# One of four weight sums per MLP unit moved from GpSimd to VectorE

## The chip, the cores and the metric

The kernel runs on one core of a Trainium2 chip. The metric is the time of one launch on the device, in microseconds, as the median of three runs.

## The reference, cut to what matters

A transformer stack on 512 tokens of width 1024, all in float32: a first block of two attention layers, then a second block of four layers whose mixers are attention, neighbourhood attention, a convolution module and a Fourier mixer. Each layer of the second block ends in the same MLP, and the change touches nothing else:

```
def sq_relu_mlp(h, w1, w2):
    return jnp.square(jax.nn.relu(h @ w1)) @ w2
...
x = x + ml[5] * sq_relu_mlp(modulate(rms_norm_2(x, norm2_g[i]), ml[3], ml[4]), mlp_w1[i], mlp_w2[i])
```

`w1` is 1024 x 4096 and `w2` 4096 x 1024. In layer 0 the MLP is applied to 256 context tokens too.

## The kernel before, in words

TensorE, VectorE, ScalarE and GpSimd each have one program, written out in full when the kernel is built, and they meet by semaphores. The work is a list of stages. Between most stages every engine has a gate that waits until the others are done with the stage before; TensorE has no gate in front of an MLP.

**An MLP stage** (kind `fast`) multiplies matrices by Strassen's method in Winograd's form: a product of 2 x 2 blocks takes seven block products and not eight. It is cut into units. A unit takes one block of weights out of a ring of three slots in SBUF (2 MB each, filled by SyncE's queue), as four sub-blocks `a11, a12, a21, a22`. The seven products want four sums of them:

- `s1 = a21 + a22`, `s2 = s1 - a11`, `s4 = a12 - s2`, made on VectorE by `weight_sums` (L2415, L2417, L2419), each into a buffer of its own, with a wait for the one before;
- `a11 - a21`, the third sum, made on GpSimd by `third_sum` (L3057), which writes it over `a21` in the ring. It waits for `s1`, since `s1` reads `a21`.

TensorE (L1856) takes a unit's products in the order 1, 5, 2, 6, 3, 7, 4 (`ORDER`), or 1, 2, 5, 6, 3, 7, 4 in a first unit. Product 5 wants `s1`, 6 wants `s2`, 3 wants `s4`, and 7 wants the third sum (`s3_made`). VectorE makes a unit's sums while TensorE is still in the unit before: behind `sum_u2` (L2484), which reads product 6 of that unit, and ahead of `c12` (L2490) and `sum_u3` (L2500). Then come `c21_sum` (L2506) and, in some units, the partial sums for the next layer's modulation (L2587, L2591). In the first unit of each kind VectorE also makes four sums of the activations (`token_sums`, L2438 to L2448). GpSimd's own list in a unit is the third sum of the next unit and then the addition that makes `c22` (L3082).

**The sizes.** Layer 0 has 32 units with sub-blocks of 128x512 elements. Layers 1, 2 and 3 have 16 units each, with sub-blocks of 128x1024. That makes 80 units.

**The start of an MLP.** The first unit's `weight_sums` has nothing ahead of it in its own stage, so it is run in the stage before, as a step named `wsums` behind one residual tile. In layers 1 to 3 that is the last tile but one of the residual additions: VectorE makes the first unit's sums and then adds the last tile (L2633 in layer 1, L2636 and L2637 in layers 2 and 3). Behind the last tile come its squares on ScalarE (L2236), their addition on GpSimd (L3030), the sum over channels on TensorE (L1682), the root on ScalarE (L2245), its inverse on VectorE (L2833, L2834), the spread on TensorE (L1696), the scaling of the second half of the tokens (L2849) with the shift on ScalarE (L2258), and the first activation sum (L2438). In the first unit TensorE goes through product 1, L1682, the first half of product 2, L1696, the second half of product 2, and product 5, which waits for L2438. GpSimd's `third_sum` of a first unit stands behind GpSimd's gate, so it runs when the MLP's stage has begun.

Of the kernel before, what the change touches and what calls it, by code (L numbers as in the profile page):

```python
# [17 lines left out]
ALU = mybir.AluOpType  # L18
# [246 lines left out]
def build_program(nc, dram, out_dram, stages_kept=10000):  # L265
    ctx = ExitStack()
    with ctx:
# [3 lines left out]
        def sem(name):  # L271
            return ctx.enter_context(nc.semaphore(name))
# [84 lines left out]
        product_ready, s_sums, s3_made, t_made = sem("product_ready"), sem("s_sums"), sem("s3_made"), sem("t_made")  # L357
# [7 lines left out]
        stages, blocks = [], []  # L365
# [203 lines left out]
        for c0 in range(0, 2560, 512):  # L569
# [8 lines left out]
        idx_tiles[2].after = [("swap", idx_heads, 0), ("swap", idx_heads, 1)]  # L578
        wi_tiles[-1].after = [("swap", idx_heads, 2)]
        ab_list = [t for _, tiles, _ in ab_groups[1:] for t in tiles]  # L580
        qk_data = ([(QA[:, t], V("qa_g")) for t in range(4)] + [(KA[:, 0], V("ka_g"))]
                   + [(QB[:, t], V("qb_g")) for t in range(4)] + [(KB[:, 0], V("kb_g"))])
# [487 lines left out]
        def shaped(x, u):  # L1070

            x = x[:, 0:u["cols"]]
            return x.rearrange("p (m n) -> p m n", m=2) if u["mt"] == 2 else x
# [390 lines left out]
        def gate(eng, own, s):  # L1464

            for name, sm in stage_of.items():
                eng.wait_ge(sm, s)
            if tables_before[s]:
                eng.wait_ge(tables_in, tables_before[s])
# [917 lines left out]
        def _(dve):  # L2387
# [19 lines left out]
            def weight_sums(u):  # L2407

                a11, a12, a21, a22 = u["blocks"]
                s1, s2, s4 = u["s"]  # L2410
                base = 3 * u["id"]
                dve.wait_ge(weights_in[u["b"] % RING], landed[u["b"]])
                if u["id"] >= 2:
                    dve.wait_ge(product_ready, 7 * u["id"] - 7)
                nc.vector.tensor_tensor(s1, a21, a22, ALU.add).then_inc(s_sums, 1)  # L2415
                dve.wait_ge(s_sums, base + 1)
                nc.vector.tensor_tensor(s2, s1, a11, ALU.subtract).then_inc(s_sums, 1)  # L2417
                dve.wait_ge(s_sums, base + 2)
                nc.vector.tensor_tensor(s4, a12, s2, ALU.subtract).then_inc(s_sums, 1)  # L2419
                sums_ahead[0] = u["id"] + 1  # L2420
# [461 lines left out]
            def next_sums(unit, _):  # L2882
                weight_sums(unit)
# [114 lines left out]
        def _(pool):  # L2998
# [38 lines left out]
            for s, st in enumerate(stages):  # L3037
                if st["kind"] not in ("prep", "norm"):
                    gate(pool, "pool", s)
                if st["kind"] == "norm":  # L3040

                    for k in range(1, st["summed"]):
                        pool.wait_ge(squares_ready, st["sq0"] + k + 1)
                        if k > 1:
                            pool.wait_ge(pool_steps, pool_count)
                        ins = nc.gpsimd.tensor_tensor(st["sq"][:, 0, :], st["sq"][:, 0, :], st["sq"][:, k, :], ALU.add)
                        if k < st["summed"] - 1:
                            ins.then_inc(pool_steps, 1)
                            pool_count += 1
                        else:  # L3050
                            ins.then_inc(sumsq_ready, 1)
                if st["kind"] == "fast":

                    def third_sum(u):
                        a11, _, a21, _ = u["blocks"]
                        pool.wait_ge(s_sums, 3 * u["id"] + 1)
                        nc.gpsimd.tensor_tensor(a21, a11, a21, ALU.subtract).then_inc(s3_made, 1)  # L3057

                    us, tmp = st["units"], st["tmp"]
                    last = us[-1]  # L3060
                    listed = {p: [x for x in last["after"][p] if x[0] == "nsq"] for p in last["order"] if p in last["after"]}
                    third_sum(us[0])
                    for i, u in enumerate(us):
                        if i + 1 < len(us):
                            third_sum(us[i + 1])
                        n_units = u["id"]
                        if u["last"]:
                            for kind, normed, at in listed[1] + listed[2] + listed[4]:
                                sum_squares(normed, *at)
                        if u.get("closes"):  # L3070
                            for kind, normed, at in [x for x in us[-2]["after"][1] if x[0] == "nsq"] + listed[1]:
                                sum_squares(normed, *at)
                        pool.wait_ge(u3_out, n_units + 1)
                        pool.wait_ge(t5_copied, n_units + 1)
                        if u["up"]:
                            to = u["dst"][1][1]
                        else:
                            to = tmp["v"][:, 0:u["cols"]]
                            if n_downs:
                                pool.wait_ge(x22_out, n_downs)  # L3080
                            n_downs += 1
                        nc.gpsimd.tensor_tensor(to, shaped(tmp["u3"], u), shaped(tmp["t5"], u),  # L3082
                                                ALU.add).then_inc(c22_out, 1)
                        if u["last"]:
                            for kind, normed, at in listed[5] + listed[3]:
                                sum_squares(normed, *at)
                        if u.get("closes"):
                            for kind, normed, at in listed[2]:
                                sum_squares(normed, *at)
                    pool.wait_ge(c22_out, us[-1]["id"] + 1)  # L3090
                if "loads_bias" in st:
                    load_bias(0)
                for dst, src, i in st.get("shifts", []):
                    values = st["groups"][-1][1]
                    pool.wait_ge(*values[i].done)
                    pool.dma_start(dst, src).then_inc(shifted_in, 16)
                if st["kind"] == "project":
                    rotations = [x for _, tiles, _ in st["groups"] for t in tiles for x in t.after] + st.get("steps", [])
                    last = None
                    for kind, job, i in rotations:  # L3100
                        if kind == "nsq":
                            sum_squares(job, *i)
                        if kind == "glu":
                            pool.wait_ge(*job.done)
                            u = U[:, i, TAPS // 2:TAPS // 2 + S]
                            nc.gpsimd.tensor_tensor(u, u, SIG[:, i, :], ALU.mult).then_inc(glu_done, 1)  # L3106
                        if kind != "swap":
                            continue
                        data, g, made_by = job.tiles[i]
                        r = job.r[i]  # L3110
                        if last is None:
                            pool.wait_ge(tables_in, tables_before[s] + 16 * len(st["loads"]))
                        if g is not None:
                            pool.wait_ge(yn_ready, job.sp[i] + 1)
                            src = job.yn[:, r % 2, 0:job.n]
                        else:
                            if made_by is not None:
                                pool.wait_ge(*made_by.done)
                            src = data
                        if r >= 2:  # L3120
                            pool.wait_ge(rope_done, r - 1)
                        nc.gpsimd.tensor_tensor(job.t1[:, r % 2, 0:job.n], src, job.cos[0:job.parts, 0:job.n],
                                                ALU.mult).then_inc(cos_ready, 1)
                        last = r + 1
                    if last is not None:
                        pool.wait_ge(cos_ready, last)
                if st["kind"] == "attention" and st["passes"][0]["bias"] is not None:
                    for t in range(1, len(st["passes"])):
                        if t >= 2:
                            pool.wait_ge(bias_used, t - 1)  # L3130
                        load_bias(t)
                pool.sem_inc(stage_of["pool"], 1)
# [89 lines left out]
```

## Time and profile before

| what | value |
|---|---|
| median of three runs | 3859.96 us (3858.89 to 3861.55) |
| span of the profiled execution | 3863.2 us |
| mean granted TensorE clock in it | 0.991 of full speed |
| TensorE matmul, weight load | 3731.4 us (97%), 2529.2 us |
| VectorE, ScalarE, GpSimd | 1986.4 us (51%), 968.1 us, 585.1 us |
| instructions | 42209 |

The span is that of one profiled execution, and no time of its own is given beside it; it is 3.2 us above the median of the runs. Durations below come from that execution. An engine's share of busy time says only how full it is. What a change of its work is worth is read from the waits of the engine that is never idle.

### The profile page before, as it was taken

The numbers are of one execution on the slowest core, as the hardware profiler recorded it, in microseconds if no ns is written. First come the engines' busy times: TensorE is split into PE (matmuls) and PEld (weight loads), VectorE is DVE, ScalarE is ACT, GpSimd is POOL, SyncE is SP. The second block draws the span as 40 slices with busy tenths as digits, with TensorE's granted clock in tenths as the row PEclk, the third lists the DMA queues.
The fourth block names the chain that finished last, engine by engine and source line by source line (L and its number), as shares of the span: only waits on it lengthen the run. The fifth ranks groups of instructions, "written<-read, shape, count | busy, mean of one in ns | idle before, by whom it ended". The sixth has DMA issues, their size and how long they took to land.

```text
span 3863.2 us, 42209 instructions
## 1 busy us (share of the span) xinstructions
PE 3731.4 (97%) x16228; PEld 2529.2 (65%) x16232; DVE 1986.4 (51%) x3470; ACT 968.1 (25%) x2234; POOL 585.1 (15%) x476
## 2 busy tenths in 40 slices
PE   9999999999999999999999899999999999999997
PEld 4458445455554655555644588888568888788886
DVE  3654346644773575564301946663765665344343
ACT  2142215521552312112201622021313111221010
POOL 1001000001000111111202411112422111111111
PEclk9999999999999999999999999999999999999998
DMA  3112331022002132333213314543102454122221
GB/s 138 62 43 89 101 106 60 1 93 72 26 1 64 66 122 96 131 109 109 72 67 81 60 44 165 183 153 109 66 22 99 163 175 153 61 73 84 87 85 43
DMA packets 226949, 341.41 MB, mean 88 GB/s; under 512 B 32256, under 2 KB 100512, under 8 KB 226720
## 3 DMA queue, kind: packets, MB, share of 16 engines
q1 hardware_dynamic: 201552, 320.60, 24.2%
q0 software_dynamic: 6816, 10.01, 1.4%
q10 hardware_dynamic: 18384, 8.11, 0.7%
q8 instruction: 132, 2.16, 0.2%
q14 instruction: 65, 0.53, 0.0%
HBM read 333.03 MB, written 4.06 MB: 87 GB/s over the span
## 4 chain that ended last, share of the span: by engine, by line
PE 88%; DVE 6%; ACT 2%; issue 2%; POOL 1%; DMA 1%; ACTq 0%; DVEq 0%; POOLq 0%
PE psum L1856 43%; PE psum L1603 29%; PE psum L1976 3%; PE psum L1923 3%; PE psum L1953 2%; PE psum L1710 1%; DVE small L2918 1%; DVE arena L2591 1%; ACT arena L2347 1%; POOL arena L3106 1%; PE psum L1632 1%; PE psum L1644 1%; PE psum L1661 1%; ACT arena L2335 1%; PE psum L1550 1%
## 5 line engine op out<-in xcount | busy, mean ns | idle before, releaser
L1603 PE MATMUL psum<-HC,ring 128*128 128x256 f32 (+2 forms) x3184 | 1034.1, 484 | 11.7 <-ACT HC L2258 4.5
L1603 PEld LDWEIGHTS psum<-HC,ring 128*128 128x128 f32 (+1 forms) x3184 | 600.1, 190 | 429.2 <-issue 375.2
L1856 PE MATMUL psum<-arena,ring 128*128 128x256 f32 (+1 forms) x2304 | 604.9, 416 | 6.0 <-ACT arena L2110 6.0
L1856 PEld LDWEIGHTS psum<-arena,ring 128*128 128x128 f32 x2304 | 433.6, 190 | 150.3 <-ACT arena L2110 10.9
L1856 PE MATMUL psum<-arena 128*128 128x256 f32 (+1 forms) x1792 | 472.3, 418 | 0.4
L1856 PE MATMUL psum<-HC,ring 128*128 128x256 f32 (+1 forms) x1792 | 435.6, 396 | 4.4 <-ACT arena L2110 4.4
L1856 PEld LDWEIGHTS psum<-arena 128*128 128x128 f32 x1792 | 340.3, 190 | 114.7 <-ACT arena L2115 0.7
L3057 POOL TENSOR_TENSOR ring<-ring 128x1024 f32<-128x1024 f32 (+1 forms) x80 | 217.2, 2715 | 1213.9 <-DVE arena L2415 1183.1
L1856 PEld LDWEIGHTS psum<-HC,ring 128*128 128x128 f32 x1792 | 338.4, 191 | 80.1 <-ACT arena L2110 5.1
L2591 DVE SCALAR_TENSOR_TENSOR arena<-ring,cond,arena 128x512 f32<-128x512 f32 x448 | 318.6, 749 | 8.0
L2484 DVE TENSOR_TENSOR arena<-psum,arena 128x384 f32<-128x384 f32 (+2 forms) x80 | 44.5, 556 | 378.1 <-PE psum L1856 378.0
L2918 DVE TENSOR_REDUCE small<-psum 128x1 f32<-128x512 f32 (+8 forms) x352 | 186.8, 565 | 92.8 <-PE psum L1935 57.8
L2335 ACT ACTIVATE arena<-psum,small 128x256 f32<-128x256 f32 (+8 forms) x320 | 183.4, 577 | 113.7 <-DVE small L2918 78.9
L3030 POOL TENSOR_TENSOR arena<-arena 128x256 f32<-128x256 f32 (+1 forms) x82 | 68.3, 833 | 926.7 <-ACT arena L2236 924.4
L2419 DVE TENSOR_TENSOR arena<-ring,arena 128x1024 f32<-128x1024 f32 (+1 forms) x80 | 201.7, 2521 | 2.7
L1953 PE MATMUL psum<-ident,arena 128*128 128x128 f32 x984 | 150.2, 282 | 34.9 <-ACT arena L2347 23.6
L1856 PE MATMUL psum<-CX,arena 128*128 128x256 f32 x768 | 175.0, 382 | 5.8 <-DVE CX L2438 5.8
L2063 ACT ACTIVATE arena<-psum 128x512 f32<-128x512 f32 (+4 forms) x124 | 58.7, 476 | 457.9 <-PE psum L1603 452.9
L1856 PEld LDWEIGHTS psum<-CX,arena 128*128 128x128 f32 x768 | 146.9, 192 | 27.1 <-issue 6.9
L2110 ACT ACTIVATE arena<-psum 128x384 f32<-128x384 f32 (+2 forms) x80 | 39.1, 489 | 485.5 <-PE psum L1856 485.5
L2347 ACT ACTIVATE arena<-psum 128x512 f32<-128x512 f32 (+3 forms) x272 | 139.7, 552 | 67.7 <-PE psum L1953 67.4
L1953 PEld LDWEIGHTS psum<-ident,arena 128*128 128x128 f32 x984 | 105.9, 142 | 74.5 <-issue 31.8
(236 smaller groups left out, 3834.1 us busy)
## 6 DMA issues: line engine op xcount, KB each, us to landing
ring<-in_mlp_w SPq DMA_DIRECT2D x64, 2048.0 KB, 8.8
ring<-in_ada_w SPq DMA_DIRECT2D x48, 2048.0 KB, 7.9
ring<-in_na_qkv SPq DMA_DIRECT2D x6, 2048.0 KB, 7.9
ring<-in_ab_in SPq DMA_DIRECT2D x5, 2048.0 KB, 9.3
ring<-in_cd_in SPq DMA_DIRECT2D x4, 2048.0 KB, 10.0
ring<-in_pw SPq DMA_DIRECT2D x8, 1024.0 KB, 6.6
ring<-in_at_qkv SPq DMA_DIRECT2D x3, 2048.0 KB, 10.4
ring<-in_ab_out SPq DMA_DIRECT2D x2, 2048.0 KB, 7.8
```

Source lines behind the costliest of these rows:

```text
L1603: last = nc.tensor.matmul(out, lhs, rhs, start=(k == 0), stop=(k == len(t.pairs) - 1))
L1856: last = nc.tensor.matmul(bank(at, u["T"], u["T"] * m), w[:, i, P * m:P * m + P], x[:, i, :], start=(opens and m == 0 and i == 0), stop=(i ...
L1923: last = nc.tensor.matmul(psum[:, at:at + k1 - k0], p["q"](g, qt * P, qt * P + P), p["k"](g, a * P + k0, a * P + k1), start=(m < 3), stop= ...
L1953: last = nc.tensor.transpose(psum[0:rows, c0:c0 + P], pair["probs"][g][:, k0:k0 + rows], ident[:, :])
L1976: last = nc.tensor.matmul(psum[HD * g:HD * g + HD, at + q0:at + q1], p["v"](g, of[0] if of else kt), chunk["turned"][0:p["krows"], kt, g, ...
L2335: nc.scalar.activation(pair["probs"][g][:, 0:nk + more], psum[:, off:off + nk + more], ACT.Exp, bias=small[:, c:c + 1], accum_out=small[:, ...
L2347: nc.scalar.activation(dst, src, ACT.Copy).then_inc(act_copied, 1)
L2419: nc.vector.tensor_tensor(s4, a12, s2, ALU.subtract).then_inc(s_sums, 1)
L2591: ins = nc.vector.scalar_tensor_tensor(partial[:, v, :], w[:, k, :], cond[:, k, v:v + 1], partial[:, v, :], ALU.mult, ALU.add)
L2918: nc.vector.tensor_reduce(small[:, c:c + 1], psum[:, off:off + nk], AX, ALU.max, negate=True).then_inc(negmax_ready, 1)
L3030: ins = nc.gpsimd.tensor_tensor(total, total, normed.sq[:, k, cols], ALU.add)
L3057: nc.gpsimd.tensor_tensor(a21, a11, a21, ALU.subtract).then_inc(s3_made, 1)
```

## The change

The third sum is issued on VectorE, in `weight_sums`, between `s2` and `s4`, with the same operands, the same place in the ring and the same semaphore. `third_sum` and its two calls are taken out of GpSimd's program. No wait is added.

```diff
@@ weight_sums, VectorE
                 nc.vector.tensor_tensor(s1, a21, a22, ALU.add).then_inc(s_sums, 1)
                 dve.wait_ge(s_sums, base + 1)
                 nc.vector.tensor_tensor(s2, s1, a11, ALU.subtract).then_inc(s_sums, 1)
+                nc.vector.tensor_tensor(a21, a11, a21, ALU.subtract).then_inc(s3_made, 1)
                 dve.wait_ge(s_sums, base + 2)
                 nc.vector.tensor_tensor(s4, a12, s2, ALU.subtract).then_inc(s_sums, 1)
@@ the MLP stages, GpSimd
-                    def third_sum(u):
-                        a11, _, a21, _ = u["blocks"]
-                        pool.wait_ge(s_sums, 3 * u["id"] + 1)
-                        nc.gpsimd.tensor_tensor(a21, a11, a21, ALU.subtract).then_inc(s3_made, 1)
...
-                    third_sum(us[0])
                     for i, u in enumerate(us):
-                        if i + 1 < len(us):
-                            third_sum(us[i + 1])
```

## Rows read from the trace of the kernel before

**Rows 1.** The page: busy time, share of the span and instructions of each engine.

```profile
PE 3731.4 (97%) x16228; PEld 2529.2 (65%) x16232; DVE 1986.4 (51%) x3470; ACT 968.1 (25%) x2234; POOL 585.1 (15%) x476
```

**Rows 2.** TensorE's waits, whole span: line <- releaser, total us, times, longest.

```profile
PE psum L1856 <- ACT arena L2110: 10.5, 12, 4.1
...
PE psum L1856 <- DVE CX L2438: 5.8, 3, 1.9
...
PE psum L1682 <- POOL arena L3030: 1.4, 2, 0.7
```

**Rows 3.** Four MLP stretches (1283.7-1880, 2302-2695, 2945-3341, 3454-3844) summed: us, busy by engine.

```profile
sum 1775.30, PE 1756.44 PEld 1357.03 DVE 954.28 ACT 300.87 POOL 324.99; mean PE 439.11 PEld 339.26 DVE 238.57 ACT 75.22 POOL 81.25
```

**Rows 4.** Groups of the sums: shapes, count, busy us, mean ns, idle before.

```profile
L2419 DVE TENSOR_TENSOR arena<-ring,arena 128x1024 f32<-128x1024 f32 (+1 forms) x80 | 201.7, 2521 | 2.7
...
L2417 DVE TENSOR_TENSOR arena<-arena,ring 128x1024 f32<-128x1024 f32 x48 | 60.0, 1250 | 1.6
...
L2417 DVE TENSOR_TENSOR arena<-arena,ring 128x512 f32<-128x512 f32 x32 | 22.1, 692 | 1.1
```

**Rows 5.** Timeline, one unit of layer 1: start, duration, engine, operation, idle before.

```profile
2311.08 3.39 POOL L3057 TENSOR_TENSOR ring<-ring 128x1024 f32<-128x1024 f32 x1 [14.24 <-DVE arena L2415]
...
2312.30 3.25 DVE L2419 TENSOR_TENSOR arena<-ring,arena 128x1024 f32<-128x1024 f32 x1
```

**Rows 6.** Timeline at the start of layer 2's MLP.

```profile
2937.97 0.54 DVE L2636 TENSOR_SCALAR arena<-psum,vec,mods 128x256 f32<-128x256 f32 x1
...
2939.49 0.72 POOL L3030 TENSOR_TENSOR arena<-arena 128x256 f32<-128x256 f32 x1 [3.79 <-ACT arena L2236]
...
2940.18 2.35 POOL L3057 TENSOR_TENSOR ring<-ring 128x1024 f32<-128x1024 f32 x1
...
2940.36 0.58 PE L1682 MATMUL psum<-mean_d,arena 128*128 128x1 f32 x4 [0.70 <-POOL arena L3030]
...
2940.80 1.97 PE L1856 MATMUL psum<-HC,ring 128*128 128x256 f32 x8
...
2941.57 1.24 DVE L2834 SCALAR_TENSOR_TENSOR sd_rstd<-ident,sd_rstd 128x256 f32<-128x256 f32 x1
...
2942.95 0.67 PE L1696 MATMUL psum<-sd_rstd,mean_d 128*128 128x256 f32 x2 [0.18 <-DVE sd_rstd L2834]
...
2943.66 1.65 DVE L2849 SCALAR_TENSOR_TENSOR HC<-X,sgain,psum 128x256 f32<-128x256 f32 x4 [0.86 <-PE psum L1696]
```

**Rows 7.** Timeline at the start of layer 1's MLP.

```profile
2292.81 0.48 DVE L2633 SCALAR_TENSOR_TENSOR X<-psum,mods,X 128x256 f32<-128x256 f32 x1
...
2293.81 0.72 POOL L3030 TENSOR_TENSOR arena<-arena 128x256 f32<-128x256 f32 x1 [3.26 <-ACT arena L2236]
...
2295.91 1.99 PE L1856 MATMUL psum<-HC,ring 128*128 128x256 f32 x8 [0.35 <-ACT arena L2110]
...
2297.74 0.59 PE L1696 MATMUL psum<-sd_rstd,mean_d 128*128 128x256 f32 x2
...
2298.37 2.05 DVE L2849 SCALAR_TENSOR_TENSOR HC<-X,sgain,psum 128x256 f32<-128x256 f32 x5 [1.25 <-PE psum L1696]
...
2302.00 7.15 PE L1856 MATMUL psum<-CX,arena 128*128 128x256 f32 x32 [1.94 <-DVE CX L2438]
```

**Rows 8.** Timeline ahead of the joint MLP of layer 0.

```profile
1263.56 0.69 DVE L2834 SCALAR_TENSOR_TENSOR sd_rstd<-ident,sd_rstd 128x512 f32<-128x512 f32 x1
...
1265.66 1.02 PE L1696 MATMUL psum<-sd_rstd,mean_d 128*128 128x512 f32 x2
```

**Rows 9.** Timeline inside layer 2's MLP, where a block of weights lands late.

```profile
3232.69 3.26 DVE L2419 TENSOR_TENSOR arena<-ring,arena 128x1024 f32<-128x1024 f32 x1
...
3243.53 3.72 PE L1856 MATMUL psum<-arena,ring 128*128 128x256 f32 x16 [1.33 <-ACT arena L2110]
```

**Rows 10.** Layer 3's MLP start: timeline, then its window: us, busy, PEclk, DMA.

```profile
3454.25 8.83 PE L1856 MATMUL psum<-CX,arena 128*128 128x256 f32 x32 [1.94 <-DVE CX L2438]
...
3454.00:3465.00 11.00, 10.75 (x42) 9.22 (x43) 6.62 (x10) 3.01 (x6) 0.00 (x0) 0.84 0.01 1
```

## The prediction

> **What bounds the kernel now.** I read four views in this order. The page's busy times [rows 1] show TensorE full, VectorE at half and GpSimd at 15%: the change takes work off an engine that is nearly empty and puts it on one with room. The table of windows over the four MLPs [rows 3] shows how closed they are: of 1775.3 us TensorE is busy for 1756.4, and VectorE for 954.3. So work on VectorE costs or gives nothing unless TensorE waits for it. The list of TensorE's waits says where that is [rows 2]. Of the sums themselves there is no row: TensorE never waits for L2415, L2417, L2419 or L3057. The waits that touch VectorE or GpSimd are three for L2438 (5.8 us) and two for L3030 (1.4 us), and the timelines put all five at the starts of the MLPs of layers 1, 2 and 3 [rows 6, 7, 10]. The twelve for L2110 are ScalarE's copy of product 1; one of 4.1 us is at the joint MLP's start, one is 1.33 us long [rows 9], and the other ten share 10.5 - 4.1 - 1.3 = 5.1 us, some 0.5 us each, which is the copy itself. So the change is to be priced at the starts and at that 1.33, and in the other units only if it made something late.
>
> **The units, 80 times.** Added on VectorE: one TENSOR_TENSOR of the form of L2417, 1.25 us for 128x1024 (48 times) and 0.69 us for 128x512 (32 times) [rows 4]. Removed from GpSimd: L3057, 3.39 us in a unit [rows 5]. There is a third effect. L2419 took 3.25 us for what L2417 does in 1.25: it began at 2312.30 and ended at 2315.55, 1.08 us after L3057 ended at 2314.47 [rows 5]. It stood behind GpSimd. Without L3057 it should take 1.25, so the four sums take 4 x 1.25 = 5.0 us, where the three took 1.25 + 1.25 + 3.25 = 5.75 (taking L2415 as L2417). The added instruction is more than paid for. `s1` and `s2` come when they did. The third sum ends 1.25 us after `s2`, 3.75 us after the start of `s1`, where L3057, which begins as `s1` ends, ended 1.25 + 3.39 = 4.64 us after it, and `s4` is 0.75 us earlier. Nothing behind them is later. Over 80 units VectorE's L2419 (201.7 us) becomes two times the busy time of L2417 (2 x 82.1 = 164.2), 37.5 us less in all, and TensorE waited for none of it. I price the units at 0, with one exception.
>
> The exception is [rows 9]. A block landed late, the sums began late, a set of activation sums came behind them, and VectorE reached L2490 so late that ScalarE's queue held up L2110: TensorE waited 1.33 us where the copy alone costs some 0.5. L2419 took 3.26 us there, and two operations of 1.25 stand in its place: VectorE is 0.76 us earlier, and the excess is 0.8. **-0.76 us.** The bounds are 0 (something else ends last there) and -0.8 (the whole excess).
>
> **The starts of layers 1 to 3.** Here the third sum is moved past other work. It was behind GpSimd's gate; now it stands on VectorE ahead of the last residual tile, and the chain square, L3030, L1682, L2833, L2834, L1696, L2849, L2438 hangs on that tile. The tile's addition moves by 1.25 us (L2419 there has no L3057 beside it yet, so nothing comes back in this place).
>
> Layer 2 [rows 6]: L1682 already waits 0.70 us for L3030, so the whole 1.25 goes through, to 2941.61. The first half of product 2 follows 0.44 behind, at 2942.05. L1696 follows that by 2297.74 - 2295.91 = 1.83 where nothing else holds it [rows 7]: 2943.88. In between something is given back: L2834 took 1.24 us beside L3057, and a tile twice as wide took 0.69 without it [rows 8]. By that way L1696 could begin at 2941.57 + 1.25 + 0.69 + 0.14 (as it began 0.14 after L2834 ended) = 2943.65, earlier than 2943.88: TensorE's own order rules. L2849 follows L1696 by 0.63 [rows 7]: 2944.51, against 2943.66. **+0.85.** Everything behind, up to product 5, hangs on L2849. Layer 3 has the same order and the other of the two waits of 0.7 us for L3030 [rows 2]; I take it as the same: **+0.85.**
>
> Layer 1 [rows 7]: L3030 ended at 2294.53, before TensorE wanted it. Now it ends at 2295.78. L1682 follows by 0.15 (as 2940.21 to 2940.36 in [rows 6]) and the product by 0.44: 2296.37 against 2295.91. **+0.46.** Bounds for the three: 0, if some wait behind takes it all up, and 3 x 1.25 = 3.75, if nothing does.
>
> The Trainium skill, page "VectorE: DVE Perf Modes", section "The TRN2 errata", has a table by which a VectorE operation from SBUF to SBUF costs 58 cycles plus its elements at 0.96 GHz, which would be 1.13 us for 1024 elements; the trace has 1.25 from one to the next, so it does not agree here. By the table the starts would cost about 0.1 us less each.
>
> Layer 0 [rows 8]: `weight_sums` runs ahead of L2833. 0.69 us more moves the end of L2834 from 1264.25 to 1264.94; L1696 begins at 1265.66 with no wait, behind a tile of matmuls that covers it. Price 0; were that cover gone, 0.69. GpSimd's L3057 had stood behind the gate there and beside L2445, which no product waited for.
>
> **Sum**: 0.85 + 0.85 + 0.46 - 0.76 = +1.40 us, 0.04% of the span of 3863.2. I take the difference over to the median of the runs: 3859.96 + 1.40 = 3861.4. Here 0.2% is 7.7 us, about what a measurement of this kernel can tell from no change.
>
> **The rivals.**
>
> A. *TensorE's clock falls more often.* Behind the 1.94 us wait of layer 3 the same 32 matmuls took 8.83 us that took 7.15 in layer 1 behind the same wait, and the granted clock of the stretch was 0.84 [rows 10, 7]: part of it at 1.2 and not 2.4 GHz, for 1.68 us. So one of three such idle spells brought a fall. The change makes idle spells of 0.70 us ahead of L1682 into 1.95 in layers 2 and 3, as long as those. For: they are new and long enough. Against: two of three passed without. With one or two more falls: 3861.4 + 1.7 to 3.4 = 3863.1 to 3864.8.
> The Trainium skill, page "TensorE: Matmul & The Clock Gate", Part 1, has the clock set by how busy the engine has been of late; the stretch at 0.84 behind an idle spell agrees, and the level in layer 1 shows that an idle spell of this length need not do it.
>
> B. *Nothing, or a little gained.* L2834 and its neighbours free of L3057 give back what the tile loses, or layer 3's fall does not recur. Against: TensorE's own order comes later than L2834 in my sums. Time: 3859.96 + 0 to -2, 3858 to 3860.
>
> C. *VectorE was the bound after all.* If TensorE's progress hung on VectorE, the 37.5 us would come through: 3822.5. Against: no row in which TensorE waits for a sum, and 1756.4 of 1775.3 us busy [rows 3]. It decides only if a fifth of it (7.7 us) reached TensorE.
> The Trainium skill, page "GPSIMD Engine Reference", section "When to use GPSIMD", would have elementwise work on VectorE because GpSimd is about twice as slow there; the trace agrees (2.35 us for L3057 beside almost nothing, 1.25 on VectorE), but the rule speaks of an instruction and not of the time of this kernel.
>
> D. *Slower by more than 0.2%.* The mechanism of A at its worst: each of the three starts has a fall behind the wait for L1682 and one behind the wait for L2438, six against the one of now, five more: 1.4 + 5 x 1.68 = 9.8, 3869.8. It decides from four more on (1.4 + 6.7 = 8.1). Layer 1's wait for L1682 hardly grows, which speaks against it.
>
> **How the numbers follow.** The forecast 0.50, A 0.25, B 0.18, C 0.03, D 0.04. The first three hold 0.93 within 0.2%. Faster is C, slower D. The range: down to B's middle and half the spread of the runs below it, 3857.6, and up to A's end with the same, 3866.2. It contains both bounds of the starts (+3.75 less nothing, 3863.7) and of the exception.
>
> **What would show it.** Right: L2419 at 1.25 us for 128x1024 and 0.69 for 128x512, no L3057; four sums of 5.0 us; L1682 in layers 2 and 3 waits 1.9 to 2.0 us for L3030, and in layer 1 under 1; L1696 waits for nothing; L2834 at 0.69 or less; L2438 waits still 1.9 us each; the wait at 3243.53 down to about 0.55; VectorE's busy time down by some 37 us, though it has 80 instructions more (82.1 us for the added ones, 119.6 less for L2419). Wrong: a wait of product 5, 6, 3 or 7 for a sum, a residual tile in time with L1682 waiting as before, or a time of more than 7.7 us either way with no wait to show for it, which only another share of half clock would explain.

## The result: 0.13% slower, and the forecast too low

| | kernel before | changed kernel |
|---|---|---|
| median of 20 runs each, in turn | 3861.97 us | 3866.72 us |
| lowest to highest | 3855.91 to 3867.38 | 3861.83 to 3870.76 |
| mean | 3861.93 us | 3866.47 us |
| ratio, 95% interval | | 1.0013 [1.0007, 1.0019] |

The change costs 3866.72 - 3861.97 = 4.75 us, by the interval 2.7 to 7.3. That is under 0.2%, as forecast, but the interval leaves the forecast's +1.40 out, and 3866.72 lies 0.5 us above the range. The miss of 3866.72 - 3861.4 = 5.3 us has two parts: 2.0 is the base (three runs had a median of 3859.96, twenty have 3861.97), and 3.35 is the effect (4.75 against 1.40). Only the second needs an explanation.

The profiled execution of the changed kernel took 3867.0 us, with a span of 3864.8. Its page, busy times first, against [rows 1]:

```profile
span 3864.8 us, 42209 instructions
...
PE 3732.6 (97%) x16232; PEld 2528.8 (65%) x16232; DVE 1931.7 (50%) x3550; ACT 967.6 (25%) x2234; POOL 367.9 (10%) x396
```

VectorE has 80 instructions more and is 54.7 us less busy; GpSimd has 80 fewer and 217 us less. The groups of the four sums, shapes apart (count, busy us, mean ns, idle before), against [rows 4]:

```profile
L2418 DVE TENSOR_TENSOR ring<-ring 128x1024 f32<-128x1024 f32 x48 | 58.5, 1218 | 0.0
...
L2420 DVE TENSOR_TENSOR arena<-ring,arena 128x1024 f32<-128x1024 f32 x48 | 58.4, 1218 | 0.0
...
L2417 DVE TENSOR_TENSOR arena<-arena,ring 128x512 f32<-128x512 f32 x32 | 22.1, 692 | 1.1
```

The groups' engine times add up to 41 us less for the sums (L2419's 201.7 became 80.3, and L2418 is 80.4). Another 13 of the 54.7 are overlap: the third sum and `s4` each start some 0.08 us before the sum ahead of them ends, and the page counts shared time once. L2418 is the third sum, and L2420 is `s4`, which was L2419. It took 3.25 us beside GpSimd's sum [rows 5] and takes 1.22 now. TensorE's waits (total us, times, longest), against [rows 2]:

```profile
PE psum L1856 <- ACT arena L2110: 9.3, 11, 4.1
...
PE psum L1856 <- DVE CX L2439: 4.9, 3, 1.9
...
PE psum L1682 <- POOL arena L3031: 3.9, 3, 1.7
```

No wait names a sum. The waits for ScalarE's copy are 1.2 us less (what that owes to the change is taken up below). The last line is what the change brought: 1.4 us in two waits became 3.9 in three. The timeline has the third of these at layer 1's start, and in layer 2 the wait that was 1.33 us long in [rows 9]:

```profile
2299.28 0.58 PE L1682 MATMUL psum<-mean_d,arena 128*128 128x1 f32 x4 [0.47 <-POOL arena L3031]
...
3247.75 2.43 PE L1856 MATMUL psum<-arena,ring 128*128 128x256 f32 x10 [0.47 <-ACT arena L2110]
```

The start of layer 2's MLP in the timeline, against [rows 6]:

```profile
2938.33 1.63 DVE L2417 TENSOR_TENSOR arena<-arena,ring 128x1024 f32<-128x1024 f32 x1
...
2939.89 1.21 DVE L2418 TENSOR_TENSOR ring<-ring 128x1024 f32<-128x1024 f32 x1
2941.03 1.21 DVE L2420 TENSOR_TENSOR arena<-ring,arena 128x1024 f32<-128x1024 f32 x1
2942.16 0.53 DVE L2637 TENSOR_SCALAR arena<-psum,vec,mods 128x256 f32<-128x256 f32 x1
...
2944.55 0.58 PE L1682 MATMUL psum<-mean_d,arena 128*128 128x1 f32 x4 [1.72 <-POOL arena L3031]
2944.99 2.85 PE L1856 MATMUL psum<-HC,ring 128*128 128x256 f32 x8
2945.76 0.42 DVE L2835 SCALAR_TENSOR_TENSOR sd_rstd<-ident,sd_rstd 128x256 f32<-128x256 f32 x1
2947.64 1.06 PE L1696 MATMUL psum<-sd_rstd,mean_d 128*128 128x256 f32 x2
...
2952.36 7.14 PE L1856 MATMUL psum<-CX,arena 128*128 128x256 f32 x32 [1.55 <-DVE CX L2439]
```

The third sum takes the place 1.14 us long ahead of `s4` (2939.89 to 2941.03), the tile comes later by it, and L1682 waits 1.72 us where it waited 0.70. L2835 takes 0.42 us where it took 1.24. Then comes what the sum of the forecast had not: the eight matmuls at 2944.99 take 2.85 us for 1.97, and L1696 takes 1.06 for 0.59 in the same form of [rows 7]. Two windows of that trace (busy us per engine in the order PE, PEld, DVE, ACT, POOL, then granted clock and DMA) show the clock there and at layer 3's start:

```profile
2945.20:2949.00 3.80, 3.80 (x12) 3.04 (x12) 0.86 (x3) 0.23 (x1) 0.00 (x0) 0.60 0.30 115
...
3451.00:3456.00 5.00, 4.80 (x15) 3.54 (x13) 2.42 (x7) 1.93 (x5) 0.00 (x0) 0.66 0.06 22
```

TensorE never stood still in the first 3.80 us and was granted 0.60 of full speed, so most of it at 1.2 and not 2.4 GHz, right behind the longer wait. The second is a fall at layer 3's start. The kernel before had one in that start too, but behind the wait of 1.94 us for L2438, in product 5 [rows 10]. Here it stands further ahead, behind the new wait:

```profile
3449.55 0.58 PE L1682 MATMUL psum<-mean_d,arena 128*128 128x1 f32 x4 [1.72 <-POOL arena L3031]
3449.98 2.68 PE L1856 MATMUL psum<-HC,ring 128*128 128x256 f32 x8
```

So both new waits of this trace have a fall right behind them, and no wait for product 5 has one.

### The profile page after: what moved, and what is told of

Its sections match the earlier page's. It is cut to its first block, busy times and chain, and to the rows that moved or that the text cites. A ratio compares the mean times of both kernels' runs of the same rounds, so it can differ in the third digit from the quotient of the medians.

```text
span 3864.8 us, 42209 instructions
## 1 busy us (share of the span) xinstructions
PE 3732.6 (97%) x16232; PEld 2528.8 (65%) x16232; DVE 1931.7 (50%) x3550; ACT 967.6 (25%) x2234; POOL 367.9 (10%) x396
## 3 DMA queue, kind: packets, MB, share of 16 engines
q8 instruction: 132, 2.16, 0.2%
## 4 chain that ended last, share of the span: by engine, by line
PE 89%; DVE 5%; ACT 2%; issue 2%; POOL 1%; DMA 0%; ACTq 0%; DVEq 0%; POOLq 0%
PE psum L1856 44%; PE psum L1603 29%; PE psum L1976 3%; PE psum L1923 3%; PE psum L1953 2%; PE psum L1710 1%; DVE small L2919 1%; DVE arena L2592 1%; ACT arena L2347 1%; POOL arena L3099 1%; PE psum L1632 1%; PE psum L1644 1%; PE psum L1661 1%; ACT arena L2335 1%; PE psum L1550 1%
## 5 line engine op out<-in xcount | busy, mean ns | idle before, releaser
L3075 POOL TENSOR_TENSOR arena<-arena 128x384 f32<-128x384 f32 (+2 forms) x80 | 79.7, 996 | 1643.4 <-DVE arena L2501 1638.0
L1603 PE MATMUL psum<-ring,HC 128*128 128x256 f32 (+2 forms) x480 | 149.0, 470 | 2.5 <-ACT HC L2258 2.5
```

Of the source, the lines that this page charges most:

```text
L1603: last = nc.tensor.matmul(out, lhs, rhs, start=(k == 0), stop=(k == len(t.pairs) - 1))
```

## The experiments

All were timed in five rounds (11 runs each, 7 of e6_twice) against 27 to 33 runs of the kernel before on the same chip; their medians were 3859.33 (first four), 3860.27 (next four), 3860.0 (next four) and 3858.67 (last three). The table gives the ratio, the difference of the means, and three parts of it. Clock: the mean granted clock of the runs before less that of the version, times 3860 us; it prices a half-speed stretch as if TensorE were busy all through it. Outside: the change in own time less span (1.79 us before). Rest: what is left. A difference of means is good to 1.3 to 2.0 us either way (two standard errors), to 2.9 in e3 and e6 and 2.4 in e4. The 95% intervals of the ratios are wider, 3.5 us either way for most. By them only e0, e4, e5, e6, e11 and e14 are clear of no change; e1, e3, e7 and e8 are not.

| version | ratio [95%] | us | clock | outside | rest |
|---|---|---|---|---|---|
| e0_change | 1.0014 [1.0005, 1.0023] | +5.0 | 3.0 | 0.4 | 1.5 |
| e1_first_only | 1.0007 [0.9998, 1.0015] | +3.1 | 2.0 | 0.0 | 1.1 |
| e2_others_only | 0.9996 [0.9987, 1.0005] | -1.0 | -0.5 | 0.0 | -0.5 |
| e3_third_late | 1.0003 [0.9994, 1.0012] | +1.0 | 2.0 | 0.4 | -1.4 |
| e4_fill | 1.0021 [1.0013, 1.0030] | +8.4 | 1.0 | 0.4 | 7.0 |
| e5_before_fill | 1.0013 [1.0004, 1.0022] | +6.4 | 3.5 | 0.0 | 2.9 |
| e6_twice | 1.0033 [1.0022, 1.0044] | +13.4 | 10.0 | 0.4 | 2.9 |
| e7_spread | 1.0001 [0.9993, 1.0010] | +1.5 | 3.5 | 0.4 | -2.4 |
| e8_fill_short | 1.0008 [0.9999, 1.0017] | +3.4 | 1.9 | 0.4 | 1.1 |
| e9_before_fill_short | 0.9998 [0.9989, 1.0007] | -1.1 | 0.1 | 0.0 | -1.2 |
| e10_late_fill | 0.9999 [0.9990, 1.0007] | -0.2 | 0.5 | 0.4 | -1.1 |
| e11_delay_only | 1.0017 [1.0008, 1.0025] | +6.3 | 3.3 | 0.0 | 3.0 |
| e12_others_fill | 1.0002 [0.9993, 1.0011] | +0.5 | 0.6 | 0.0 | -0.1 |
| e13_spread_fill | 0.9999 [0.9990, 1.0008] | +0.1 | 1.3 | 0.4 | -1.6 |
| e14_half_delay | 1.0012 [1.0003, 1.0021] | +5.3 | 4.1 | 0.0 | 1.2 |

A "fall" is a stretch in which TensorE was granted half its clock. "Start" below is the stretch from the first matmul of product 1 of a layer's MLP to the end of the 32 matmuls of products 5 and 6. Undisturbed, meaning less the 1.7 us of a fall where one lies in it, the three take 17.55 + 18.38 + 18.38 = 54.31 us in the trace of the kernel before.

**The change, and its two halves.** The first three versions are the change again, the change for the first unit of each MLP alone, and for all the others alone. `chase` marks the first unit of an MLP, of which there are four. e2 also makes VectorE wait for the third sum of the unit before. The halves differ from the kernel before by:

```diff
 # e1: from the kernel before
+                if u["chase"]:
+                    nc.vector.tensor_tensor(a21, a11, a21, ALU.subtract).then_inc(s3_made, 1)
...
-                    third_sum(us[0])
+                    if not us[0]["chase"]:
+                        third_sum(us[0])
 # e2: from the kernel before
+                if not u["chase"]:
+                    dve.wait_ge(s3_made, u["id"])
+                    nc.vector.tensor_tensor(a21, a11, a21, ALU.subtract).then_inc(s3_made, 1)
...
-                        if i + 1 < len(us):
-                            third_sum(us[i + 1])
```

> The changed kernel again, as the measure for the three runs beside it. Both theories: ratio to before near 1.0013, that is +3 to +7 us. First theory (the starts): the three residual tiles are 1.14 us later, which adds about 2.2 us by itself, and longer idle spells ahead of L1682 bring more stretches at half clock (1.7 us each). Second theory (the units): VectorE's 77 further sums slow something in the ordinary units.

> Only the first unit of each MLP has its third sum on VectorE, the other 76 stay on GpSimd. First theory: all of the loss is there, ratio 1.001 to 1.0018 (+4 to +7 us), L1682 waits 1.7 us in layers 2 and 3 and the wait in layer 2 (1.33 us in the kernel before) is as before. Second theory: the loss is gone, ratio 0.9995 to 1.0003.

> The other part alone: 76 units have their third sum on VectorE, the first unit of each MLP keeps it on GpSimd. First theory: no loss, ratio 0.9995 to 1.0002, with the 1.33 us wait in layer 2 down to about 0.6. Second theory: all of the loss, ratio 1.001 to 1.0018.

The timeline of e0 at the starts of layers 2 and 3:

```profile
2939.27 0.58 PE L1682 MATMUL psum<-mean_d,arena 128*128 128x1 f32 x4 [1.72 <-POOL arena L3031]
...
2947.47 7.14 PE L1856 MATMUL psum<-CX,arena 128*128 128x256 f32 x32 [1.94 <-DVE CX L2439]
...
3452.43 7.14 PE L1856 MATMUL psum<-CX,arena 128*128 128x256 f32 x32 [1.94 <-DVE CX L2439]
```

Of e1 and e2, at the start of layer 2:

```profile
2939.91 0.58 PE L1682 MATMUL psum<-mean_d,arena 128*128 128x1 f32 x4 [1.72 <-POOL arena L3032]
...
2943.39 1.05 PE L1696 MATMUL psum<-sd_rstd,mean_d 128*128 128x256 f32 x2
```

```profile
2938.87 0.58 PE L1682 MATMUL psum<-mean_d,arena 128*128 128x1 f32 x4 [0.70 <-POOL arena L3033]
```

e1 has the starts of e0 to 0.1 us, with the longer wait and the slow L1696 behind it, and +3.1 us, below the +4 to +7 expected. e2 keeps the starts of the kernel before, has 76 of the 80 sums moved, and -1.0 us. e0 and e2 are 6.0 +/- 2.2 apart, so the loss sits with the first units, and the other 76 sums cost nothing, as priced. (The two halves add up to 2.1 against 5.0 for the whole. 0.4 of that gap is a term outside the span that only the whole has, see below; the other 2.5 is just inside the error of these differences, 2.6, and wasn't resolved.) One expectation for e1 failed in a telling way: it had the 1.33 us wait of [rows 9] stay, and the wait was 0.47. That is taken up under the exception below. e0, the same kernel as the changed one, shows that falls move from one execution to another: it has one behind L1682 at 2940.1 as that one had, but none at layer 3's start, where the 32 matmuls take 7.14.

The undisturbed starts of e0 are 17.73 + 18.97 + 18.97 = 55.67 us, +1.36 against the forecast's 0.46 + 0.85 + 0.85 = 2.16.

**The third sum taken off the tile's path.** In e3 the first unit's third sum is issued at the start of VectorE's MLP code, behind the tile; the other units are as in the changed kernel.

```diff
+                if not u["chase"]:
                     nc.vector.tensor_tensor(a21, a11, a21, ALU.subtract).then_inc(s3_made, 1)
@@ fast(st), VectorE
+                a11, _, a21, _ = us[0]["blocks"]
+                nc.vector.tensor_tensor(a21, a11, a21, ALU.subtract).then_inc(s3_made, 1)
```

> All third sums on VectorE, but that of a first unit is issued behind the gate, at the start of the MLP, where VectorE waits 2.4 us for ScalarE's root. First theory: last residual tile and L1682 as in the kernel before, L2834's form at 0.42 us, ratio 0.9990 to 1.0001 (0 to 4 us less than before). Second theory: the loss stays, ratio 1.001 to 1.0018. The third sum in that gap could also delay L2834 if the gate opens late; then L1696 waits more than 0.2 us.

Its timeline at layer 2's start:

```profile
2937.94 0.58 PE L1682 MATMUL psum<-mean_d,arena 128*128 128x1 f32 x4 [0.70 <-POOL arena L3034]
...
2940.19 0.59 PE L1696 MATMUL psum<-sd_rstd,mean_d 128*128 128x256 f32 x2
...
2944.45 7.15 PE L1856 MATMUL psum<-CX,arena 128*128 128x256 f32 x32 [1.94 <-DVE CX L2440]
```

The wait is 0.70 again, L1696 is at full speed, and the starts sum to 53.48, 0.83 below the kernel before. All four sums of every unit are on VectorE here, as in the changed kernel, and the difference to the kernel before is +1.0 +/- 2.9, where e0 has +5.0. e3 alone is a weak measure (its runs go from 3855.4 to 3867.9 us, and e0 is 4.0 +/- 3.1 above it), but e10 and e13 below have the same sums off the tile's path and are at -0.2 and +0.1. What costs is the place ahead of the tile, not the engine.

**Delay without the change.** Two kernels hold the delay apart from the engine. e11 is the kernel before with `s4` of the first units of layers 1 to 3 computed twice; its third sums are on GpSimd. e6 is the changed kernel with the same doubling.

```diff
                 dve.wait_ge(s_sums, base + 2)
+                if u["chase"] and u["mt"] == 2:
+                    chain(nc.vector.tensor_tensor(s4, a12, s2, ALU.subtract))
                 nc.vector.tensor_tensor(s4, a12, s2, ALU.subtract).then_inc(s_sums, 1)
```

> The changed kernel with one more VectorE operation of 1.2 us (s4 made twice) ahead of the last residual tile in layers 1 to 3. If the starts are what costs, each is 1.1 to 1.2 us longer again: +3.4 us against the changed kernel, ratio to before 1.0018 to 1.0030, and L1682 waits 2.9 us in layers 2 and 3. If the starts cost nothing, ratio as the changed kernel, 1.0007 to 1.0018.

> The kernel before, third sums on GpSimd, with one more VectorE operation of 1.2 us (s4 made twice) ahead of the last residual tile in layers 1 to 3. If it is the delay of the tile and not where the third sum is made: L1682 waits 0.5, 1.7 and 1.7 us, ratio as with only the first units changed, 1.0004 to 1.0016. L2834 still beside GpSimd's L3057, so up to 0.5 us a start more. If the delay costs nothing: 0.9996 to 1.0003.

> The kernel before with one more VectorE operation of 0.69 us (the half of s4 made twice) ahead of the last residual tile in layers 1 to 3: L1682 waits about 1.4 us in layers 2 and 3. By delay alone: 3 starts of 0.2 to 0.5 us each, +1 us, ratio 1.0001 to 1.0005. If idle spells of 1.4 us bring falls of the clock already: +2 to +4 us, ratio 1.0005 to 1.0011, with a stretch at half clock behind L1682 in the trace.

e14 is e11 with the doubled subtraction over half of `s4`. TensorE's waits for the tile, in e6, e11 and e14:

```profile
PE psum L1682 <- POOL arena L3033: 7.7, 3, 3.0
```

```profile
PE psum L1682 <- POOL arena L3032: 4.6, 3, 2.0
```

```profile
PE psum L1682 <- POOL arena L3032: 3.1, 3, 1.4
```

The doubled delay costs 13.4 us where the single one costs 5.0, above the range expected for longer starts (ratio 1.0018 to 1.0030, at most 11.6 us). The three starts of its trace take 64.7 us as they stand, against 56.0 in the trace of the kernel before with its one fall. Its starts of layers 2 and 1 as windows:

```profile
2946.00:2952.00 6.00, 3.93 (x11) 3.38 (x12) 1.23 (x4) 1.37 (x4) 0.72 (x1) 0.67 0.44 171
...
2296.00:2306.00 10.00, 6.67 (x24) 4.99 (x24) 4.75 (x11) 3.47 (x9) 0.72 (x1) 0.83 0.40 152
```

In e6 all three starts hold half-speed stretches, and 10.0 of the 13.4 us stand with a lower mean granted clock (0.9886 against 0.9912). The line of e11 at layer 2, with its window:

```profile
2945.05 0.58 PE L1682 MATMUL psum<-mean_d,arena 128*128 128x1 f32 x4 [1.96 <-POOL arena L3032]
```

```profile
2946.00:2950.00 4.00, 4.00 (x12) 3.23 (x11) 1.91 (x4) 0.00 (x1) 1.20 (x1) 0.57 0.12 47
```

e11 makes the whole loss (+6.3) with nothing moved between engines, and again a stretch of 4.00 busy us at 0.57 behind a wait of 1.96. With L3057 still beside L2834's form, nothing is given back: its starts, undisturbed, are 57.1 us, 2.8 more than in the kernel before. e14 has waits of 1.43, starts of 56.1 us (+1.8), and lost 5.3, though no start of its trace holds a fall: there the dose does not follow the wait's length, and the loss is above both expectations.

**Filling the waits.** If the waits bring the falls, matmuls of constants inside them should stop these. The versions put N matmuls of `mean_d` ahead of L1682 and ahead of product 5 of a first unit, into banks that are written over later.

```diff
             def normed_sum(normed, half, busy=0):
...
                 open_bank(7)
+                for _ in range(busy):
+                    nc.tensor.matmul(bank(7), mean_d[:, :], mean_d[:, :].unsqueeze(1).to_broadcast([P, ST, P]),
+                                     start=True, stop=True)
                 pe.wait_ge(sumsq_ready, n["sumsq"] + 1)
...
+                        if p == 5 and u["chase"] and st["split"] is not None:
+                            for _ in range(2):
+                                nc.tensor.matmul(bank(at), mean_d[:, :], mean_d[:, :].unsqueeze(1).to_broadcast([P, ST, P]),
+                                                 start=True, stop=True)
```

The counts (ahead of L1682 in layer 1, in layers 2 and 3; ahead of product 5) and the kernels they were put into: e4 1, 3; 4 into the changed one; e5 0, 1; 4 into the one before; e8 0, 2; 2 into the changed one; e9 0, 0; 2 into the one before.

> The changed kernel, with TensorE given matmuls of constants (128x512, results overwritten) in its idle spells at the starts of layers 1 to 3: one or three ahead of L1682, four ahead of product 5's wait. Nothing waits less for data. If idle spells bring stretches at half clock, the granted clock stays at 2.4 GHz in 30 us behind each start, and the time falls by 2 to 5 us against the changed kernel (ratio to before 1.0000 to 1.0007). If the loss is the delay alone, ratio 1.0010 to 1.0018, since the matmuls take no wait away.

> The kernel before with the same filler: none or one ahead of L1682, four ahead of product 5's wait. If the falls of the clock behind these waits matter in the kernel before too, ratio 0.9990 to 0.9998 (1 to 4 us less). If the clock plays no part, 0.9998 to 1.0003.

> The changed kernel with a filler that fits: two matmuls of constants (0.86 us each) ahead of L1682 in layers 2 and 3, two ahead of product 5 in layers 1 to 3, both shorter than the waits of 1.72 and 1.94 us. If half clock behind the idle spells is part of the loss, no stretch at half clock lies within 12 us behind the starts and the time falls by 2 to 4 us against the changed kernel: ratio to before 1.0002 to 1.0009. If the delay alone is the loss: 1.0010 to 1.0018.

> The kernel before with two such matmuls ahead of product 5 in layers 1 to 3. If the clock falls behind the wait of 1.94 us in one start of three or more: 1 to 3 us less, ratio 0.9992 to 0.9998. If not: 0.9998 to 1.0004.

The fill of e4 was too long. Its timeline ahead of product 5 of layer 2:

```profile
2956.04 3.60 PE L1847 MATMUL psum<-mean_d 128*128 128x512 f32 x8
```

Four matmuls took 3.60 us in a wait of 1.94, so e4 (+8.4) and e5 (+6.4) measure mostly their own filling: their starts are 60.9 and 58.1 us, 5.2 and 3.8 more than undisturbed ones without it. e8 is the short form; layer 2's timeline, then its window:

```profile
2942.20 1.88 PE L1679 MATMUL psum<-mean_d 128*128 128x512 f32 x4
...
2948.43 1.88 PE L1847 MATMUL psum<-mean_d 128*128 128x512 f32 x4
```

```profile
2946.00:2952.00 6.00, 5.86 (x23) 4.09 (x23) 4.44 (x9) 3.30 (x8) 0.00 (x0) 1.00 0.03 11
```

The clock stays at full speed with the same late tile. None of the 21 starts in the traces of the seven filled versions holds a half-speed stretch; 5 of 12 do in the four delayed ones (the changed kernel, e0, e1, e11), 3 of 3 in e6, and 2 of 12 in those with neither (before, e2, e3, e7). e14 has none in 3. Filled against not filled, that is 0 of 21 against 10 of 30, and chance would hardly do it. The 5 of 12 against 2 of 12 it could well do. In time, e8 is +3.4 +/- 1.3 against the +5.0 of e0: less by 1.6 +/- 2.2, in the right direction and within the error. So the filling stops the stretches; that it wins back time is not shown. e9, -1.1 +/- 2.0, says that the filling by itself costs nothing that could be measured.

**Looking for a version that wins.** e7 is the changed kernel with the first unit's sums one by one behind three tiles and `s4` at the start of the MLP. e10, e12 and e13 are e3, e2 and e7 with 2 matmuls ahead of product 5.

```diff
-            return stage("project", groups=groups, sums_tile=groups[3][1][2], **kw)
+            return stage("project", groups=groups, sums_tile=groups[3][1][0:3], **kw)
...
-                            before["sums_tile"].after.append(("wsums", u, None))
+                            for x, tile in enumerate(before["sums_tile"]):
+                                tile.after.append(("wsums", u, (x + 1,)))
...
                 else:
+                    weight_sums(us[0], (4,))
                     normed_inverse(normed, 1)
```

> All sums on VectorE; the first unit's s1, s2 and third sum each behind one of the last group's first three residual tiles (gaps of 2.4 us), and s4 at the start of the MLP. The last tile waits for no sum. First theory: L1682 waits for nothing, the starts of layers 2 and 3 are 0.8 us shorter each than in the kernel before, ratio 0.9988 to 0.9998 (1 to 4 us less than before), the fastest of all. If the starts don't matter: ratio as that of the changed kernel.

> All third sums on VectorE, a first unit's behind the gate (as in the run with the late third sum), and two filler matmuls ahead of product 5. Both parts of the first theory together: starts no longer than before, no fall of the clock behind them, the wait of 1.33 us in layer 2 shortened. Ratio 0.9988 to 0.9997. If starts and clock don't matter, 1.0007 to 1.0018 as the changed kernel.

> 76 third sums on VectorE, the first unit's on GpSimd, and two filler matmuls ahead of product 5 in layers 1 to 3. If starts and clock are all: starts as before and never at half clock (0.8 us less on average), the wait in layer 2 0.8 us less: 1 to 3 us less than before, ratio 0.9992 to 0.9998. If third sums on VectorE in the ordinary units cost something through the clock elsewhere: 1.0000 to 1.0007.

> All sums on VectorE, the first unit's spread over the gaps between residual tiles, s4 behind the gate, and two filler matmuls ahead of product 5. By starts and clock: starts 0.9 us shorter each in layers 2 and 3 and never at half clock, ratio 0.9988 to 0.9996. If what is left of the loss (the run with the spread sums lost 1.5 us though its starts were shorter) hangs on having no third sum on GpSimd: 1.0000 to 1.0008, with a mean granted clock below that of the kernel before.

The timeline of e7 in layers 2 and 3:

```profile
2940.98 1.99 PE L1857 MATMUL psum<-HC,ring 128*128 128x256 f32 x8 [0.35 <-ACT arena L2111]
...
2947.07 7.14 PE L1857 MATMUL psum<-CX,arena 128*128 128x256 f32 x32 [1.94 <-DVE CX L2444]
...
3450.68 8.83 PE L1857 MATMUL psum<-CX,arena 128*128 128x256 f32 x32 [1.94 <-DVE CX L2444]
```

The wait of L1682 is gone, TensorE has only the 0.35 of the copy, and each undisturbed start is 17.53 us, 1.7 us below the kernel before over the three. Yet e7 is +1.5: its clock part is 3.5, one fall stands at 3450.68 behind the unchanged 1.94 wait, and others lie in places that have nothing to do with the MLP starts. e13 closes that wait too: the starts are down to 52.40 us, and the time is +0.1. All four versions are within the error of the kernel before, and above what they were expected to reach. None is a clear winner; e2 and e9, both at -1 +/- 2, are the lowest.

## Why the forecast was wrong

**Right.** The 80 units cost nothing: e2 has 76 of them and is at 0.9996. The chain L3030, L1682, L1696, L2849 was the path by which the third sum reached TensorE: the waits for a tile grew from 1.4 to 3.9 us, e2, e10 and e13 are without the loss when the tile is not delayed, and e11 makes it without the change. L2419 did stand behind GpSimd (3.25 to 1.22 us), L2834 was freed (1.24 to 0.42), layer 0 stayed covered, and rival C (VectorE the bound) is dead: 54.7 us less busy time of VectorE brought nothing. The forecast named 37; the sums gave 41, and most of the rest is overlap.

**Terms that were off in size.** The tile moved by 1.01 to 1.14 us, not 1.25: `s4` follows the third sum without waiting for its result. Layers 2 and 3 cost 0.59 each (0.85 forecast), layer 1 0.19 (0.46). The starts together are 1.36 us against 2.16.

**The exception, which wasn't the change's to give.** The forecast took the 1.33 us wait of [rows 9] as fixed and credited 0.76 us for it. In the changed kernel's trace the wait is 0.47, so 0.86 less, as if confirmed. But it is 0.47 in e1 too, where the third sum of that unit is still on GpSimd and `s4` (L2421 there) still takes 3.26 us. What VectorE waited for the block of weights, in the kernel before, in the changed one, and in e1 with what followed:

```profile
3230.18 1.22 DVE L2415 TENSOR_TENSOR arena<-ring 128x1024 f32<-128x1024 f32 x1 [1.72 <-DMA ring<-in_mlp_w]
```

```profile
3234.34 1.23 DVE L2415 TENSOR_TENSOR arena<-ring 128x1024 f32<-128x1024 f32 x1 [0.81 <-DMA ring<-in_mlp_w]
```

```profile
3229.97 1.23 DVE L2415 TENSOR_TENSOR arena<-ring 128x1024 f32<-128x1024 f32 x1 [0.69 <-DMA ring<-in_mlp_w]
...
3232.49 3.26 DVE L2421 TENSOR_TENSOR arena<-ring,arena 128x1024 f32<-128x1024 f32 x1
...
3243.50 3.72 PE L1856 MATMUL psum<-arena,ring 128*128 128x256 f32 x16 [0.47 <-ACT arena L2110]
```

The block landed less late. In the six traces with that third sum on GpSimd, TensorE waited 1.33 us where VectorE had waited 1.72 for the block, 0.81 where 1.19 (e11), 0.57 where 0.96 (e14), and 0.47 where 0.69 or less (e1, e5, e9). In the eleven with it on VectorE it waited 0.47 every time. By these rows TensorE would have waited 0.57 at most behind the changed kernel's 0.81 in the old order too. So nearly all of the 0.86 came from the landing and not from the change. The change is worth about 0.22 us here, an estimate: the mean of the six waits, 0.69, less 0.47. The direct terms are then 1.36 - 0.22 = about +1.1 us, against +1.40.

**A term that wasn't there.** Own time less span is 2.17 to 2.29 us in every run of the changed kernel and 1.74 to 1.86 in every run of the kernel before, 0.43 us more that no view of the span can show. It is there in each version in which GpSimd issues no third sum (e0, e3, e4, e6, e7, e8, e10, e13: means of 2.21 to 2.25) and in none in which it issues some (e1, e2, e5, e9, e11, e12, e14: 1.78 to 1.80), four of them being enough in e2. What it is, ahead of the first instruction or behind the last, is not in the traces.

**The step that failed.** The forecast of +1.40 passes the delay on with the clock as before, so its sum has no term for falls of the clock, and rival A, which has them, got half the chance. Delay, exception and the term outside come to 1.36 - 0.22 + 0.43 = 1.6 us. e0 lost 5.0, so 3.4 are left, and up to 3.0 of these stand with a lower mean granted clock, 0.9905 against 0.9913. That fits rival A and its size, "one or two more falls, 1.7 to 3.4"; with it the forecast's own sum would have been 3863.1 to 3864.8, on the base of 3861.97 some 2 more, and 3866.72 falls in it. The row that should have weighed more was [rows 10]: a 1.94 us wait of TensorE had already brought a fall, the change was to make two more such waits, and against this stood only "two of three passed without". In the four traces with the delay layer 2 had a fall behind its new wait each time, and layer 3, behind the same wait, in one of the four. The second step that failed is the exception, credited with 0.76 us and worth about 0.2. Rival B fell: some 0.4 us a start did come back in layers 2 and 3 (the wait grew by 1.02, the start by 0.59), the forecast had counted on that, and the time rose. So did D: no trace of the changed kernel shows more than two of the six falls that it needs.

How firm this is. Shown: the loss comes from the delay at the first units (e2 without it, e11 with nothing else), a longer delay costs much more than its own length (e6: the waits for the tile grew by 6.3 us and the time by 13.4), and matmuls in the waits keep the starts free of half-speed stretches (0 of 21).

Argued, not shown: that falls behind the new waits make up the 3.4 us. Three things stand against taking it as settled. The clock column is not the delay's alone: e3 and e7, which have no longer wait, are at 2.0 and 3.5, and e5 is at 3.5 with no fall in a start. Over the 122 runs of the kernel before, those at 0.990 took 3863.4 us on average, at 0.991 3860.5, at 0.992 3858.2, at 0.993 3856.8, some 2.2 us for each 0.001, where the column takes 3.9; the recorded values are rounded to 0.001, so the column is an upper figure, and by the slope e0's share is about 1.8. And e8, with the waits filled, is not clearly faster than e0.

Open: 0.4 us of e0 by the column, 1.6 by the slope, that none of these terms holds, and where the extra falls sit. The traces can't say: the first product of layer 0's MLP begins at 1276.88 us in the kernel before and at 1280.45 in the changed one, and at 1276.9 to 1282.9 in the 17 traces, though the work ahead of it is the same but for one 0.7 us sum. One execution differs from the next there by more than the whole effect, so a pair of spans does not carry the comparison, and only the means over runs do. e14 lost 4.1 by the clock column with no fall at the starts of its one trace, and e7 3.5 with one.

## What to carry to other kernels

When an edit lengthens an idle spell of TensorE, price the spell and, separately, a fall of the clock behind it, and look in the kernel's own trace for a spell of the new length: if one of three had a fall of 1.7 us, two new ones are worth an expected 1.1 us (an estimate). Moving work between engines is free or not by its place in the queue, not by the engine: the same four sums on VectorE cost 5 us ahead of the residual tile and nothing measurable behind it. Don't credit a change with a wait that one trace shows behind a transfer: look whether the transfer is as late in a second execution. Give a difference, not a time, when the base is a median of three: here 2.0 of the 5.3 us were that.

## What the runs showed of the hardware

- Half-speed stretches came in lengths of 3.4 us, or twice that (layer 2 of e6), at the MLP starts; one of 3.4 cost 8.83 - 7.15 = 1.7 us. The kernel before had 11 stretches below full speed in its trace, 70.7 us of its span in all, and the changed one 13, 72.3 us. The changed one had four, at 235.7, 491.7, 2700.2 and 2945.9 us, with none near them in the other, and only the last is at an edited place; the kernel before had two such, at 2874.3 and 3382.9. So a count in one trace proves little.
- A matmul of 128x512 f32 from constants took 0.90 to 0.94 us and stands as two records in the trace (4 took 3.60 us, 2 took 1.88).
- A VectorE sum of 128x1024 took 1.22 us on average, and one that doesn't wait for the result of the sum ahead of it (`s4` behind the third sum) starts 1.14 us behind that one's start.
- The same block of weights, wanted at the same place of the program, kept VectorE waiting for 0.69 us in one trace (e1) and 1.72 in another (the kernel before), and TensorE behind it for 0.47 and 1.33.
- The 0.43 us outside the span (1.79 to 2.23), above.
